# Trimmed token ranges behind the second attention, and six merged insertions in the first attention

## The reference

```
# layer 1 of the second block; T = 16 meta tokens + 512
mix = fox_mixer(hn, b_w_q, b_w_out, k_sh, v_sh, c_sh)       # causal attention
h = h + rmsnorm(mix, g[1])
ff = conv_ffn(rmsnorm(h, g[2]), ffn_w_up, ffn_conv, ffn_w_down)
h = h + rmsnorm(ff, g[3])
return h[:, N_META:]

def conv_ffn(x, w_up, conv_w, w_down):
    u = causal_dwconv(x @ w_up, conv_w)      # 3 taps: token t reads t-2, t-1, t
    gate, val = jnp.split(u, 2, axis=-1)
    return (jax.nn.silu(gate) * val) @ w_down
```

```
for g in range(3):  o_g, lse_g = attention of group g (windows of 64 steps of 1, 4, 16 tokens)
o = sum over g of softmax(lse)_g * o_g       # = sum(exp(s) v) / sum(exp(s)) over all three
```

## Time and profile before

| | before |
|---|---|
| median of 3 runs | 3845.82 us (3841.38 to 3847.1) |
| the profiled execution's own time | 3846.73 us |
| its span | 3844.7 us |
| mean granted TensorE clock | 0.976 of full |
| PE busy | 3685.3 us (96%) |
| DVE busy | 1951.2 us (51%) |
| ACT busy | 1329.8 us (35%) |
| POOL busy | 151.6 us (4%) |
| HBM read | 308.27 MB, 81 GB/s over the span |

### The profile page before, as it was taken

One profiled execution on the slowest core, in us unless ns is written; L12 is line 12 of the kernel. 1 busy time (PEld: TensorE's weight loads), 2 busy tenths in 40 slices (PEclk: granted clock), 3 DMA queues, 4 the chain that ended last, 5 costly groups with the idle time before them and its releaser, 6 DMA issues. The chain is left out here.

```text
span 3844.7 us, 57861 instructions
## 1 busy us (share of the span) xinstructions
PE 3685.3 (96%) x22661; PEld 3224.8 (84%) x22661; DVE 1951.2 (51%) x2813; ACT 1329.8 (35%) x1980; POOL 151.6 (4%) x180
## 2 busy tenths in 40 slices
PE   8999899999999999999899989988999899889998
PEld 7888788888888887787788869988999887689998
DVE  3334853335333666666733345555664355656653
ACT  3222542224222433333432235544333333333332
POOL 1000010001000100000100010001000100010001
PEclk9999999999999999999899989989999999989999
DMA  4233222332333222221133322211223221012232
GB/s 134 95 104 96 91 83 89 105 102 77 98 98 102 79 66 72 66 72 61 55 94 98 104 66 72 67 55 61 93 87 99 66 73 39 28 55 88 93 99 72
DMA packets 89985, 312.71 MB, mean 81 GB/s; under 512 B 10832, under 2 KB 15312, under 8 KB 89696
## 3 DMA queue, kind: packets, MB, share of 16 engines
q1 hardware_dynamic: 89344, 308.24, 24.7%
q0 software_dynamic: 480, 2.17, 0.2%
HBM read 308.27 MB, written 2.10 MB: 81 GB/s over the span
## 5 line engine op out<-in xcount | busy, mean ns | idle before, releaser
L624 PE MATMUL ps<-x_hi,w_hi 128*128 128x264 f32 (+2 forms) x3952 | 1351.7, 342 | 14.1 <-DVE x_lo L1980 6.5
L624 PE MATMUL ps<-x_hi,w_lo 128*128 128x264 f32 (+2 forms) x3952 | 1334.8, 338 | 0.0
L624 PE MATMUL ps<-x_lo,w_hi 128*128 128x264 f32 (+2 forms) x3952 | 1331.1, 337 | 0.0
L1672 DVE TENSOR_TENSOR w_lo<-raw,w_hi 128x1024 fp32r<-128x1024 f32 x579 | 706.4, 1228 | 361.4 <-ACT w_hi L1155 352.4
L624 PEld LDWEIGHTS ps<-x_hi,w_hi 128*128 128x128 f32 x3952 | 746.2, 189 | 118.0 <-issue 23.9
L624 PEld LDWEIGHTS ps<-x_lo,w_hi 128*128 128x128 f32 x3952 | 744.7, 188 | 80.6
L624 PEld LDWEIGHTS ps<-x_hi,w_lo 128*128 128x128 f32 x3952 | 746.3, 189 | 77.6
L624 PE MATMUL ps<-h_hi,w_hi 128*128 128x264 f32 (+2 forms) x1992 | 650.4, 327 | 6.1 <-issue 3.9
L624 PE MATMUL ps<-h_hi,w_lo 128*128 128x264 f32 (+2 forms) x1992 | 641.2, 322 | 0.0
L624 PE MATMUL ps<-h_lo,w_hi 128*128 128x264 f32 (+2 forms) x1992 | 639.3, 321 | 0.0
L1155 ACT ACTIVATE w_hi<-raw 128x1024 fp32r<-128x1024 f32 x579 | 602.9, 1051 | 103.2 <-PE ps L624 95.3
(11 more groups left out here) (229 smaller groups left out, 3163.6 us busy)
## 6 DMA issues: line engine op xcount, KB each, us to landing
raw<-wstream SPq DMA_DIRECT2D x579, 512.0 KB, 3.4
res<-xT SPq DMA_DIRECT2D x8, 256.0 KB, 7.4
out<-res SPq DMA_DIRECT2D x4, 264.0 KB, 2.2
invc<-consts POOLq DMA_DIRECT2D x1, 1024.0 KB, 5.6
out<-res SPq DMA_DIRECT2D x4, 248.0 KB, 2.1
bias<-consts POOLq DMA_DIRECT2D x1, 512.0 KB, 3.8
g_chunk<-consts POOLq DMA_DIRECT2D x1, 264.0 KB, 3.0
g_keep<-consts POOLq DMA_DIRECT2D x1, 256.0 KB, 3.1
```

What stands on the lines that cost most here:

```text
L624: m = pe.matmul(ps[:, bank, 0:n], w[:, slot, wt, :], x[:, k, c0:c0 + n], start=first and q == 0, stop=last and q == 2)
L1672: dve.tensor_tensor(w_lo[:, slot], raw[:, slot], w_hi[:, slot].bitcast(F32), ALU.subtract)\
```

## The change

In numbers: TAIL = 516 tokens (4 + 512). `project2` behind `fox` and the inputs of the last `glu2` work on the last 516 columns, as two halves of 258; the convolution and all behind it, with the last `project2`, work on the 512 real tokens, in one bank where whole tiles are computed and in halves of 256 where the halves are computed in turn. In `attend1` the stationary tile of `weigh` is 64 columns wide, v or ones; outputs of both heads go to bank 6 (head 0 on partitions 0-63, head 1 on 64-127) and both sums to bank 7; all of a pair is weighed in one insertion, and the insertions are at slots 6, 14, 34, 51, 59 and 70. DVE copies the values in one instruction and normalises both heads in one reciprocal and one product over 128 partitions.

```diff
+TAIL = S + 4
-    project2(KD, (KD,), 4, "norm11", "norm12")
-    ffn2(1, 0, "norm13")
+    project2(KD, (KD,), 4, TAIL, "norm11", "norm12")
+    ffn2(1, 0, TAIL, S, "norm13")
...
-        val = at("val", [P, R4, 3, 3 * HD])
+        val = at("val", [P, R4, 3, P])
+        ones = at("ones", [P, HD])
...
         def two_banks(tok):
-            return tok == T
+            return tok > S
...
         def half_of(tok, h):
-            return (h * (T // 2), T // 2) if two_banks(tok) else (META + h * (S // 2), S // 2)
+            return T - tok + h * (tok // 2), tok // 2
...
-                def weigh(p, half, near):
-
-                    out = ps[:, 6 + half, :]
+                def weigh(p, near):
+
+                    def both(cols, weights, moving, start, stop):
+                        for bank, what in ((6, weights), (7, lambda half: ones[:, :])):
+                            for half in range(2):
+                                m = pe.matmul(cols(ps[head(half), bank, :]), what(half), moving(half),
+                                              start=start, stop=stop, skip_group_check=True)
+                        return m
...
-                    if t in (4, 8, 13, 18):
-                        scores_turned(p, (4, 8, 13, 18).index(t))
-                    if t == 24:
-                        weigh(p, 0, False)
-                    if t == 30:
-                        weigh(p, 0, True)
-                    if t == 33:
-                        weigh(p, 1, False)
-                    if t == 36:
-                        weigh(p, 1, True)
+                    if t == 6:
+                        turn_values(p, 2)
+                        scores_turned(p, 0)
+                        scores_turned(p, 1)
+                    if t == 14:
+                        scores_turned(p, 2)
+                        scores_turned(p, 3)
+                    if t == 34:
+                        weigh(p, False)
+                        weigh(p, True)
...
-                                if slot == 2:
-                                    turn_values(p - 1, 2)
                                 second_part(p - 1, slot)
-                            if slot in (51, 54, 57, 61):
-                                scores(p, (51, 54, 57, 61).index(slot))
+                            if slot == 51:
+                                scores(p, 0)
+                                scores(p, 1)
                             if slot == 59:
                                 turn_values(p, 0)
-                            if slot == 66:
+                                scores(p, 2)
+                                scores(p, 3)
+                            if slot == 70:
                                 turn_values(p, 1)
-                            if slot == 70:
                                 widen(p)
...
-                def normalise(p, half):
+                def normalise(p):
-                    o, total = head(half), head(1 - half)
-                    dve.wait_ge(A["pv"], 2 * p + half + 1)
-                    dve.reciprocal(recip[o, :], ps[total, 6 + half, :]).then_inc(A["rec"], 1)
+                    dve.wait_ge(A["pv"], p + 1)
+                    dve.reciprocal(recip[:, :], ps[:, 7, :]).then_inc(A["rec"], 1)
```

More of the change, by code:

```diff
@@ L695, in project @@
             def project(st):
-                chunks, tok, halved = st["chunks"], T if st["kind"] == "project2" else S, st["halved"]
+                chunks, tok, halved = st["chunks"], st["tok"], st["halved"]
                 src = x_src if st.get("source") == "x" else h_src
@@ L734, in project @@
                     squares_of(st, 0, range(squared, KD))
-                if tok == S and st["scaled"]:
+                if st["kind"] == "project" and st["scaled"]:
                     at1 = (0, 5) if halved == 1 else (0, 7)
@@ L864, in weigh @@
                             if r % 2 == 0:
[L865 to L870, removed]
+                                pe.wait_ge(A["exp"], 8 * p + r + 2)
@@ L871, in weigh @@
+                            for g in (1, 2):
+                                both(lambda out: out[:, r * P:(r + 1) * P], lambda half: val[:, r, g, head(half)],
+                                     lambda half: probT[:, half, r // 2,
+                                                        WIN * (r % 2) + P * (g - 1):WIN * (r % 2) + P * g],
+                                     (g, r) == (1, 0), False)
                         return
-                    by_r = out.rearrange("p (r i) -> p r i", r=R4)
@@ L873, in weigh @@
                     for c in (2, 3):
-                        pe.wait_ge(A["exp"], 8 * p + 2 * c + half + 1)
+                        pe.wait_ge(A["exp"], 8 * p + 2 * c + 2)
                         for at_, n, b in chunk_parts(c):
                             lo, hi = window(b)
-                            m = pe.matmul(by_r[:, :, lo // R4:hi // R4], val[:, b, 0, HD * half:HD * half + P],
-                                          probT[:, half, c, at_:at_ + n].rearrange("p (r i) -> p r i", r=R4),
-                                          start=False, stop=(c, b) == (3, 3), skip_group_check=True)
+                            m = both(lambda out: out.rearrange("p (r i) -> p r i", r=R4)[:, :, lo // R4:hi // R4],
+                                     lambda half: val[:, b, 0, head(half)],
+                                     lambda half: probT[:, half, c, at_:at_ + n].rearrange("p (r i) -> p r i", r=R4),
+                                     False, (c, b) == (3, 3))
@@ L1378, in body @@
                             act.wait_ge(s_cv, 6 * c - 3)
-                        act.activation(sbv(upad2[:, 0, 2:], T), psv(slot, T), ACT.Copy).then_inc(s_evac, 1)
+                        act.activation(sbv(upad2[:, 0, 2:], tok), psv(slot, tok), ACT.Copy).then_inc(s_evac, 1)
                         if not (isinstance(k, int) and k < 1):
@@ L1384, in body @@
                         past(act, s_cv, 6 * c)
-                        act.activation(sbv(upad2[:, 1, 2:], T), psv(slot + 1, T), ACT.Copy).then_inc(s_evac, 1)
+                        act.activation(sbv(upad2[:, 1, 2:], tok), psv(slot + 1, tok), ACT.Copy).then_inc(s_evac, 1)
                         act.wait_ge(s_cv, 6 * c + 3)
-                        act.activation(pair[:, 0, :], pair[:, 0, :], ACT.Silu).then_inc(s_gate, 1)
+                        act.activation(pair[:, 0, out], pair[:, 0, out], ACT.Silu).then_inc(s_gate, 1)
                 body(0)
@@ L1453, in square @@
                 past(act, s_sqp, st["s0"] + n - 1 if k > 1 else st["s0"] + KD * h)
[L1454 to L1455 removed]
+                c = half_cols(st["tok"], h)
+                act.activation(pair[:, k % 2, c], res[:, k, c], ACT.Square).then_inc(s_sqr, 1)
             def next_input(st, *other):
@@ L1851, in attend1 @@
             def attend1(st):
-                def head(half):
-                    return slice(HD * half, HD * half + HD)
                 def slope(p, half):
@@ L1984, in glu2 @@
                 taps = {part: [f"conv{st['l']}{part}{tap}" for tap in range(3)] for part in "gv"}
+                n_out = st["tok_out"]
+                c0 = T - n_out
+                out = slice(c0, T)
                 def convolve(part, k, c):
                     q = "gv".index(part)
-                    src, dst = upad2[:, q, :], pair[:, q, :]
+                    src, dst = upad2[:, q, c0:c0 + 2 + n_out], pair[:, q, out]
                     def tap(n):
@@ L2024, in body @@
                         dve.wait_ge(s_cv, 6 * c + 6)
-                        dve.tensor_tensor(pair[:, 1, :], pair[:, 0, :], pair[:, 1, :], ALU.mult).then_inc(s_h, 1)
+                        dve.tensor_tensor(pair[:, 1, out], pair[:, 0, out], pair[:, 1, out], ALU.mult).then_inc(s_h, 1)
                 dve.wait_ge(s_zero, 1)
```

121 lines of the change are left out of this document (59 added, 62 removed).

## The result

The changed kernel takes 3818.1 us (median of four runs, 3815.66 to 3820.53) against 3845.36 us for the kernel before: ratio 0.993, 95% interval 0.9915 to 0.9946. The forecast was 3819.8. The profiled execution has a span of 3818.1 us, 26.6 under the 3844.7 of before, where the sum said 26.0. The total agrees much better than its terms do: errors of opposite sign cancel, so I go through it stage by stage.

A forecast was written before the change was run, and what follows sets the result against it. PE was taken to set the pace, matmuls costing their columns; -13.7 us from trimming and -12.3 from the first attention make -26.0: 3820.7 us for the profiled execution, 3819.8 against the median, range 3812 to 3830.

The forecast's parts named there:

- Last projection on 512: -5.7 and -0.7: Last projection: 462 matmul pairs become single 512-column matmuls, -5.7 us; 132 matmuls in the halved tile shrink to 256 columns, -0.7.
- Inputs of the last feed-forward network: -5.7: Last network's inputs on 516 columns: 2112 matmuls, each 6 columns shorter, save 2.7 ns each, -5.7 us.
- Rival A: Stages trimmed to 516 tokens: 258 columns cost what 264 do, giving 3826.5 us; chance 0.09.
- Scores -6.4: First attention: four score insertions per pair become two, saving 2 x 0.40 us over eight pairs, -6.4 us.
- turned -5.6: First attention: turned-score insertions merged likewise, only in the seven pairs inside the stream, 2 x 0.40 us each, -5.6 us.
- turning wait -0.8: First attention: the third turning, four slots later, no longer waits for ACT's values, 0.12 us over seven pairs, -0.8 us.
- weighing +2.4: First attention: weighing in narrow tiles takes 6.93 us per pair instead of 6.6, +0.35 over seven pairs, +2.4 us.
- B: Weighing at slot 34: narrow tiles of two heads don't run side by side, +53 us over eight pairs, 3873 us; chance 0.04.
- D: First attention: the 0.40 us belongs to each score group, or a merged insertion waits, losing 12.0 us, 3832 us; chance 0.06.
- Rival C: Weighing's far groups: long runs of narrow records are held by issue, 13 us more over seven pairs, 3833 us; chance 0.03.
- End of attend1: -1.9: Uncovered end of the first attention: weighing ends about 1837.1, one normalisation of 4.4 us follows, -1.9 us.
- The wait checks (slots 14, 34, 70): Merged first-attention insertions should not wait: some 1.4 us margin at slot 14, about 2.5 at 70, exponentials ready at 34.

The follow-up runs named there:

- f1: The changed kernel with full-tile matmuls behind the second attention on 256 columns per half from columns 16 and 272, first matmul of a tile on 258; 3814.39 us.
- f2: The changed kernel with full-tile matmuls behind the second attention on 256 columns per half from columns 12 and 270, first matmul of a tile on 258; 3819.3 us.
- a2: The changed kernel run once more, unaltered; 3817.36 us.
- e4: The changed kernel with its weighing split into two insertions, far groups at slot 30 and near group at slot 34; 3818.27 us.
- e1: The changed kernel with the first attention of the kernel before, so only the trimmed ranges remain; 3831.39 us, beside 3843.88 for the kernel before.
- e5: The changed kernel with the old weighing (128-column tiles, four insertions at slots 24, 30, 33, 36, two normalisations), new score and turning slots kept; 3817.03 us.
- c1: The changed kernel with 528 tokens again behind the second attention up to the last network's inputs, full-tile matmuls on columns 8 to 264 and 264 to 528; 3822.34 us.
- n1: The changed kernel with 248 columns per half from columns 16 and 272 in the last network and projection, first product into each bank 258; 3810.5 us.
- n2: The changed kernel with 248 columns per half from columns 12 and 268 in the last network and projection; 3810.16 us.

## Why the prediction was right, and where it was not

The total was right by 0.6 us, and that close an agreement is luck: two groups of terms were mis-sized, in opposite directions, by 3.6 and 4.4 us. The mechanism held in the attention and in the last projection. For 258 columns the line through three widths did not.

*Last projection on 512: -5.7 and -0.7.* Measured -6.1, and 0.2326 us a matmul. Right.

*Inputs of the last feed-forward network: -5.7.* This is the term that failed. The whole stage moved by 2.2 us, the 1920 full-tile matmuls by 1.6 where 5.2 were due. The step took the line through 512, 264 and 256 columns and said that it holds on both sides of 258. The 256 on it was one stretch of ten matmuls. As a reading it was sound: the trace of before has 21 stretches of 50 or more matmuls of 256 columns, which start at columns 16 and 272, and in 19 of them the pace is 0.117. But it doesn't carry over to 258 from columns 12 and 270. In the last network 256 columns take 0.1170 in f1 and 0.1191 in f2, 258 columns 0.1200, 0.1197 or 0.1191, and the mean slope from 264 down to 240 is 0.35 ns per column. By that slope 6 columns are worth 2.1 ns, 4.4 us over 2112 matmuls, and the pattern an execution falls into moves the stage by another 1.6. In a2 the same 1920 matmuls gained 3.2 us. Rival A (258 costs what 264 does) is wrong too, though the first profile came near it. *Second w_out: -1.0 with -0.3 for the chain* measured -0.7, and it is of the same kind.

*Scores -6.4, turned -5.6, turning wait -0.8, weighing +2.4.* Together -10.4 up to the last widening; measured -12.0. The price of a crossing was put at 0.40; merging two insertions measured 0.41 for scores, and e4 gave 0.35 for the weighing from a separate kernel. The weighing was 6.88 against 6.93, or +0.27 a pair against the 6.60 that the old four insertions measure, where +0.35 was forecast. By pair the scores gave 1.59 (forecast 1.6), the turnings 0.17 (0.12), and the full-tile stream between the insertions some 0.11, since it ran at 0.2319 instead of 0.2325 us a matmul, which no term had. Together that is the 1.60 a pair, 0.23 over the forecast, and over seven pairs the 1.6 us that the forecast lacked. Rivals B and D are out: records of two heads overlap (0.109 a step), merging paid 0.41, and no merged insertion waits. The rule of the Trainium skill ("TensorE: Matmul & The Clock Gate", Part 3) that loads overlap only across row groups doesn't hold for these column pairs in this trace, 96 records in 6.88 us. Rival C, where issue holds narrow runs, is out as well: four records take 0.218 us, 0.054 each, over 64 in a row, against the about 81 ns that the same page of the Trainium skill gives under "Back-to-back issue gap".

*End of attend1: -1.9.* Measured -3.9 from before, but 1.2 of that is the clock, as e1 shows: with old code the tail took 29.15 there, and in e5 too. Against them the change gives -2.6 (26.51). The new tail is the same code in eleven of the executions and took 26.06 to 26.89 us, the shortest in e4, where the granted clock stayed at 1.00 through the scores and the weighing. Against e1 the weighing starts 0.3 us sooner and is 1.0 shorter (8.67 us from its first start to its last end, against 9.70), as forecast. The normalisation was undersized. I had priced the second one's end (1843.78) against a new one that starts 0.3 us behind the weighing, which makes 1.0 from weighing to projection; measured 1.4 (6.53 us from the last weighing record's end to the projection in before, 6.52 in e1, 5.17 after). Before, DVE was still at the first head when PE ended (1838.1), and began the second one's reciprocal only at 1839.34; now it begins 0.05 us behind PE's last matmul.

*The wait checks (slots 14, 34, 70).* All three held, with no releaser in any pair.

What agreed by chance: the untouched stretch between the attentions and through the second one was 1.5 us shorter. Its pieces differ between executions by up to 2.6 us either way (from the second attention's first matmul of all (on the tile f_c, line 1026 in before) to its first score 18.4 us pass in before, f2, c1, n1 and n2, and 15.8 in the change and the other runs). The four runs of the change, 3815.66, 3816.07, 3820.13 and 3820.53, spread by 4.9. What stays open is what selects a pattern in the network's stream. Neither the start column nor the width explains all the runs by itself. That the start matters at 256 columns is not excluded: f1 and f2 differ by more than two executions of one program did (0.0021 against 0.0009), but each ran once. No run separated PSUM banks, weight loads and the traffic of the other engines.

No version beat the change by more than executions differ. One that keeps the old weighing in the seven streamed pairs (e5's 1.45 us) and the new one in the last (2.5 us) should; it was not tried.

## What to carry to other kernels

Price an insertion by what it costs the stream around it (last matmul before to second one behind, less two paces): here that gave 0.35 to 0.41 us for each crossing between tile shapes, and merging insertions was worth that in every pair, while the weighing in narrow tiles cost 0.2 to 0.3 us a pair inside the stream and, with one normalisation instead of two, gave about 2.5 at the uncovered end. Price columns left out only where the tile is wide: 512 against 2 x 264 paid in full, 258 against 264 paid a third to two thirds. Before a term of one per cent of a matmul goes into a sum, see how far that stage differs between two executions of one program.

## What the runs showed of the hardware

- The pace of a stream of 258-column matmuls with a weight load each is steady within an execution (48 in 5.76 or in 5.72 us, 38 times in a row) and can be another in a second execution of the same program: 230.38 and 228.78 us for 1920.
- Paces: 512 columns 0.232 us, 264 0.1208, 256 0.1170 and 0.1191, 248 0.1147 and 0.1143, 240 0.1125. All but the 512 are from the last network. Start columns at a multiple of 64 bytes or not made no consistent difference (0.0021 less at 256, 0.0004 more at 248).
- Two matmuls of 64 output columns each, on different halves of the array's columns, with their own weight loads, take 0.109 us a pair at 128 columns, also 64 in a row.
- At the end of the first attention the same code took 30.38 us where the granted clock fell just ahead of the scores, and 29.15 in two executions where it fell some 5 us behind their start.
- Leaving the full array for half-array tiles and coming back cost 0.35 to 0.41 us an insertion, with scores in it or a weighing; 16 full-array records between two matmuls of the stream cost 0.111 each and nothing over.
